# Maxima products ahead of the value product, later query copies, an earlier first modulation block

## The chip, the cores and the metric

The kernel runs on one core of a Trainium2 chip. Its time is the device time of one execution in microseconds (us); three executions of the kernel before gave 932.08, 932.74 and 933.2 us, median 932.74. Everything is computed in 32-bit floating point: where a matrix product runs on operands rounded for TensorE (type fp32r), the rounded-off rest is kept as a second operand and multiplied too.

Five engines run side by side, each through its own list of instructions in order: TensorE (PE) multiplies and transposes, VectorE (DVE) and ScalarE (ACT) work elementwise, GpSimd (POOL) too, and SyncE (SP) issues most transfers. They wait for one another by semaphores, which the kernel sets by hand.

## The reference

Two layers of a trunk over 512 latent tokens and 256 context tokens of width 1024. Per layer:

```
shift, scale, gate = split(silu(c) @ w_mod + b_mod)        # "modulation"; the same for the context with c_ctx
h = rms_norm(x, norm_w) * (1 + scale) + shift
u = h @ w_in                                               # 22 units of 128 columns
y_a = gated linear attention, 4 heads, chunks of 64, forwards and backwards
y_b = 6 heads of latent attention (MLA): 64 + 32 query and key columns, the 32 rotated
y_c = 6 query heads over 2 key heads (GQA, "grouped"), normed and rotated
x = x + gate * (concat(y_a, y_b, y_c) @ w_out)             # the context too, in layer 0
```

The latent queries of both softmax branches look at all 768 keys, the context's (layer 0 only) at 256. The softmax subtracts the largest score of each query. At the end the latent tokens are normed once more.

## The kernel before

**Tiles and stages.** The 768 tokens are six tiles of 128. At the start, each tile of x is loaded by SP, its sum of squares and the reciprocal root are made by ACT (`x_rstd`, L702 to L708), it is scaled by DVE (`xhat`, L1109), transposed by PE (L1652, eight transposes of 128x128), and copied out of the two banks by DVE and ACT (`turned_copy`, L1133 and L750). Between them stands the modulation: the small vectors are loaded into one tile and transposed by PE (L1657), ACT and DVE make silu of c (`condition`, L761 to L768 and L1069 to L1082), and PE multiplies it with blocks of 256 scale and 256 shift columns of w_mod (`mod`, L1616). The row that comes out is copied by ACT (`mod_rows`, L671), turned by PE (`mod_turn`, L1633), and made into coefficients by DVE (`mod_cols`, L1091 to L1102). Then ACT modulates the hidden columns (`modulate`, L727), DVE splits them into a rounded part and the rest (`split_hidden`, L1161, L1163), and PE multiplies with units of w_in (`unit_products`, L1671 to L1673). A unit is also split in two parts: ACT rounds it (`unit_high`, L721), DVE subtracts (`unit_low`, L1171).

Before the change the small vectors are transposed behind tile 0, the first modulation block stands behind tile 3, and all of `unit_low` is DVE's.

**Heads.** Behind the projections stand twelve heads per layer, 0 to 5 MLA, 6 to 11 GQA. PE goes through units of one key tile by 256 or 512 queries: eight in layer 0 (two for the context's queries, then six), six in layer 1. In each unit it makes the scores (MLA: L1941 to L1943; GQA: L1947 and L1949), and two units later the value product with the exponentials (`pv`, L1894, out of `flush`). ACT makes the exponentials (L1012). Between them PE makes scores of the next head for the maxima alone (`maxes`, L1859): from unit `MAX_FROM` on (3 in layer 0, 2 in layer 1), two per unit. DVE reduces each (L1462; L1454 for the context's), joins them into negated maxima (L1466), PE transposes these at the start of the next head (`max_rows`, L1865), and DVE writes them as extra rows of the queries (L1476), so that the score product subtracts them. A grouped head has no projection of its own, an MLA head has.

The gated linear attention goes along in the heads of each layer, one tile per head: its scores are made in unit `MAX_FROM` - 1 of the head before (`gla_a`) into two banks, and DVE copies them out under a mask (`a_mask`, L1333).

**Banks.** Products go into six banks of the accumulation memory, taken in turn by `open_`; each opening waits until the group that had the bank six openings earlier has been read. Value products have two banks of their own and open none of the six.

**ACT in a head.** It makes the exponentials in the order of the units. Behind the first it makes the reciprocal of the former head's denominators in two steps (`recip`, L968 and L970). For the grouped heads it copies the next head's queries and, at some heads, keys (`gqa_in`: part 0 the rounded queries, L944, and at every second head a copy for two heads, L948; part 1 the keys, L938, for the second grouped head; part 2 the queries for the other product, L952). Before the change part 0 stands before the first exponential of a head, parts 1 and 2 behind the first and the second. In heads 8 to 10 ACT also rounds pieces of w_out (L986).

The order of the work is written out by hand in the lists of the engines; there is no planner.

Of the kernel before, what the change touches and what calls it, by code (L numbers as in the profile page):

```python
# [26 lines left out]
ALU = mybir.AluOpType  # L27
# [198 lines left out]
def build(nc, tally, a, out):  # L226
    up, dma, at, let_go = tally.up, tally.dma, tally.at, tally.let_go
    with ExitStack() as ctx:
# [245 lines left out]
        def _(pool):  # L474
# [31 lines left out]
            for l in range(DEPTH):  # L506
                if l == 0:
                    swap_small(0)
                if l == 0:
                    pool.wait_ge(*at("filled", "mod", 0, 3))  # L510
                    layer_weights(0)
# [131 lines left out]
        def _(act):  # L643
# [68 lines left out]
            for l in range(DEPTH):  # L712
# [41 lines left out]
                if l == 0:  # L754
                    for t in range(TILES):
                        x_rstd(0, [t])
                        if t % 2 == 0 and t:
                            turned_copy(t - 1)
                        if t == 2:
                            act.wait_ge(*at("vec_turned"))  # L760
                            act.activation(ct[:, 0, :], vt[:, 0:16], ACT.Abs).then_inc(*up("cond_abs"))  # L761
                            act.wait_ge(*at("cond_abs"))
                            act.activation(ct[:, 0, :], ct[:, 0, :], ACT.Exp, scale=-1.0).then_inc(*up("cond_exp"))
                            act.wait_ge(*at("cond_exp"))
                            act.activation(ct[:, 0, :], ct[:, 0, :], ACT.Ln, bias=ones[:, 0:1]).then_inc(*up("cond_ln"))
                        if t == 3:
                            act.wait_ge(*at("cond_logsig"))
                            act.activation(ct[:, 1, :], ct[:, 1, :], ACT.Exp).then_inc(*up("cond_sig"))  # L768
# [231 lines left out]
                for h in heads:  # L1000
                    todo = [(q0, nq, kt) for q0, nq, nk in qbs(l) for kt in range(nk // P)]
                    more = h + 1 < len(heads)
                    if more:
                        if h + 1 < MLA_H:
                            head_in(h + 1)
                        elif h + 1 > MLA_H:
                            gqa_in(h + 1, 0)
                    for j, (q0, nq, kt) in enumerate(todo):
# [14 lines left out]
                        if h + 1 == MLA_H and j == 1:  # L1023
                            gqa_in(h + 1, 3)
                        if j < 2 and more and h + 1 > MLA_H:
                            gqa_in(h + 1, j + 1)
                        if j == 1 and h < len(out_tiles(l)):
# [36 lines left out]
        def _(dve):  # L1064
# [80 lines left out]
            for t in range(TILES):  # L1145
                if t == 3:
                    condition(1)
                xhat(0, t)
                if t:
                    turned_copy(t - 1)  # L1150
                if t == 2:
                    condition(0)
                if t == 3:
                    condition(2)
            turned_copy(TILES - 1)

            for l in range(DEPTH):
# [16 lines left out]
                if l == 0:  # L1174
                    mod_cols(0, 0)
                    unit_low(0)
                    split_hidden(0)
# [401 lines left out]
        def _(pe):  # L1579
# [64 lines left out]

            pe.wait_ge(*at("ident_in"))
            for t in range(TILES):
                pe.wait_ge(*at("xhat", 0, t))
                for half in range(2):
# [4 lines left out]
                    close(mm, "xr", t, half)  # L1653
                if t == 0:
                    pe.wait_ge(*at("vec_in"))
                    p = open_("vec")
                    close(pe.transpose(p[:, 0:V_ROWS], vec, ident[0:V_ROWS, 0:V_ROWS]), "vec")  # L1657
                if t == 3:
                    first_mod()

            def unit_products(p, l, item, c, ks):
                slot = UNITS[UNIT_OF[item]][1]
                pe.wait_ge(*at("w_split", l, UNIT_OF[item]))
                high, low = unit_parts(l, UNIT_OF[item])
# [30 lines left out]
            for l in range(DEPTH):  # L1695
# [216 lines left out]
                for h in heads:  # L1912
# [13 lines left out]
                    for j, (q0, nq, kt, nkt) in enumerate(units):  # L1926
# [31 lines left out]
                        if m and j == MAX_FROM[l] + (-1 if m[2] < 4 else 1):  # L1958
                            mod_turn(*m[1:])
                        flush(2)  # L1960
                        if j == 0 and h < len(tiles):
# [3 lines left out]
                        if j == MAX_FROM[l] - 1 and h + 1 < len(tiles):  # L1965
                            gla_a(tiles[h + 1])
                        if j >= MAX_FROM[l]:
                            maxes(groups[:2])
# [95 lines left out]
```

## Time and profile before

| | us |
|---|---|
| median of three runs | 932.74 |
| the profiled execution, its own time | 932.37 |
| its span, first to last instruction | 930.6 |
| PE busy | 889.3 |
| DVE busy | 532.6 |
| ACT busy | 414.7 |
| POOL busy | 170.0 |

The times of the rows are those of the profiled execution, counted from the start of its span. Busy time is time in which the engine works on an instruction; PEld is the loading of weights into TensorE, which goes beside its products. The granted clock is the share of TensorE's full clock of 2.4 GHz; 0.50 is 1.2 GHz. Its mean over the span is 0.99.

### The profile page before, as it was taken

How to read it: one execution, taken by the hardware profiler on the slowest of the kernel's cores; microseconds unless marked ns; L12 is line 12 of the kernel's file. 1: busy time of each engine (PE TensorE's matmuls, PEld its weight loads, DVE VectorE, ACT ScalarE, POOL GpSimd, SP SyncE). 2: the span in 40 equal slices, each digit the busy share in tenths (PEclk: the TensorE clock that was granted, in tenths of full speed). 3: DMA queues.
4: the chain of work that ended last, by engine and by line, in shares of the span. 5: the costliest groups of instructions: out<-in, count | busy, mean ns of one | idle time of the engine just before them, and what ended most of it. 6: DMA issues, size and time to landing. Idle time of an engine off the chain costs nothing.

```text
span 930.6 us, 12648 instructions
## 1 busy us (share of the span) xinstructions
PE 889.3 (96%) x4493; PEld 649.4 (70%) x4493; DVE 532.6 (57%) x941; ACT 414.7 (45%) x771; POOL 170.0 (18%) x200
## 2 busy tenths in 40 slices
PE   3799999999999999999999999999999999999995
PEld 2488889888766665655588888889775655545584
DVE  3545634534467677767624664743646877666624
ACT  5435534321344445667731744642314435546702
POOL 1031000001362223002162000000017211002240
PEclk8899999999999999999999999999999999999998
DMA  9842220320202222222027103411402000222032
GB/s 327 266 137 56 68 70 23 92 66 4 91 1 91 92 91 91 92 91 90 1 90 208 69 4 88 108 52 40 120 4 89 0 1 1 91 91 91 0 113 91
DMA packets 76252, 74.19 MB, mean 80 GB/s; under 512 B 6340, under 2 KB 64032, under 8 KB 76064
## 3 DMA queue, kind: packets, MB, share of 16 engines
q1 hardware_dynamic: 69776, 60.24, 21.1%
q0 software_dynamic: 4016, 12.77, 3.9%
q8 instruction: 39, 0.64, 0.3%
q10 hardware_dynamic: 2400, 0.38, 0.2%
q14 instruction: 21, 0.17, 0.1%
HBM read 69.18 MB, written 4.19 MB: 79 GB/s over the span
## 4 chain that ended last, share of the span: by engine, by line
PE 88%; DVE 5%; ACT 2%; issue 2%; POOL 1%; ACTq 1%; DVEq 0%; POOLq 0%
PE pv L1894 13%; PE bank L1671 10%; PE bank L1672 10%; PE bank L1673 10%; PE bank L1982 4%; PE bank L1980 4%; PE bank L1981 4%; PE bank L1859 4%; PE bank L1825 2%; PE bank L1941 2%; PE bank L1947 2%; PE bank L1943 2%; PE bank L1942 2%; PE bank L1719 2%; PE bank L1718 2%
## 5 line engine op out<-in xcount | busy, mean ns | idle before, releaser
L1671 PE MATMUL bank<-hA_parts,W_parts 128*128 128x512 f32 (+1 forms) x480 | 173.4, 361 | 4.9 <-DVE h_low_parts L1163 4.9
L1672 PE MATMUL bank<-hA_parts,W_parts 128*128 128x512 f32 (+1 forms) x496 | 173.6, 350 | 0.0
L1012 ACT ACTIVATE hA<-bank 128x512 f32<-128x512 f32 (+1 forms) x168 | 93.7, 563 | 128.5 <-PE bank L1943 76.2
L1462 DVE TENSOR_REDUCE mxp<-bank 128x1 f32<-128x384 f32 x192 | 95.7, 549 | 29.8 <-PE bank L1859 29.4
L1671 PEld LDWEIGHTS bank<-hA_parts,W_parts 128*128 128x128 f32 x480 | 91.1, 190 | 23.5 <-issue 11.4
L1673 PE MATMUL bank<-h_low_parts,W_parts 128*128 128x512 f32 (+1 forms) x300 | 105.2, 351 | 0.0
L1672 PEld LDWEIGHTS bank<-hA_parts,W_parts 128*128 128x128 f32 x496 | 94.1, 190 | 12.8 <-issue 1.7
L1894 PE MATMUL pv<-hA,vg 128*128 128x512 f32 (+1 forms) x168 | 81.6, 571 | 3.3 <-ACT hA L1012 3.3
L1171 DVE TENSOR_TENSOR W_parts<-W,W_parts 128x1024 fp32r<-128x1024 f32 x43 | 53.9, 1254 | 38.8 <-ACT W_parts L721 38.8
L1894 PE MATMUL pv<-hA,h_low 128*128 128x512 f32 (+1 forms) x144 | 68.5, 556 | 0.0
L721 ACT ACTIVATE W_parts<-W 128x1024 fp32r<-128x1024 f32 x43 | 45.4, 1056 | 38.8 <-DMA W<-in_w_in 38.3
L1673 PEld LDWEIGHTS bank<-h_low_parts,W_parts 128*128 128x128 f32 x300 | 57.0, 190 | 7.7
L1981 PE MATMUL bank<-W_parts,hA_parts 128*128 128x512 f32 x160 | 62.3, 389 | 0.0
L813 ACT ACTIVATE tz<-bank 128x512 f32<-128x512 f32 (+1 forms) x24 | 12.6, 526 | 83.9 <-PE bank L1673 83.9
L702 ACT ACTIVATE tz<-XA 128x1024 f32<-128x1024 f32 x16 | 16.9, 1055 | 72.8 <-DVE XA L1559 72.8
L1218 DVE SCALAR_TENSOR_TENSOR YA<-tz,bank 128x512 f32<-128x512 f32 (+1 forms) x24 | 14.3, 597 | 57.3 <-ACT tz L813 57.3
L1859 PE MATMUL bank<-W_parts 96*128 96x384 f32 (+1 forms) x108 | 44.9, 493 | 1.2 <-DVE glaqk L1333 0.5
L1433 DVE SCALAR_TENSOR_TENSOR hA<-pv,hA 64x512 f32<-64x512 f32 (+1 forms) x36 | 21.5, 598 | 41.7 <-ACT hA L970 41.4
L1554 DVE TENSOR_TENSOR rt<-bank,cqkv 128x512 f32<-128x512 f32 x20 | 13.7, 687 | 54.5 <-DMA XA<-in_x 19.0
L1673 PE MATMUL bank<-rounded,W_parts 128*128 128x512 f32 (+1 forms) x120 | 41.8, 348 | 0.0
L1894 PEld LDWEIGHTS pv<-hA,vg 128*128 128x128 f32 x168 | 29.5, 190 | 16.3 <-ACT hA L1012 6.8
L533 POOL TENSOR_TENSOR XA<-XA,con 128x512 f32<-128x512 f32 x10 | 12.2, 1221 | 148.8 <-DVE XA L1315 78.3
(288 smaller groups left out, 1897.3 us busy)
## 6 DMA issues: line engine op xcount, KB each, us to landing
W<-in_w_in SPq DMA_DIRECT2D x39, 512.0 KB, 4.0
W<-in_w_mod SPq DMA_DIRECT2D x8, 1024.0 KB, 6.5
W<-in_w_mod SPq DMA_DIRECT2D x4, 2048.0 KB, 7.9
W<-in_w_out SPq DMA_DIRECT2D x4, 2048.0 KB, 7.9
gqk<-in_w_mod SPq DMA_DIRECT2D x4, 768.0 KB, 9.2
cqkv<-in_w_mod SPq DMA_DIRECT2D x4, 768.0 KB, 9.2
XA<-in_x SPq DMA_DIRECT2D x4, 512.0 KB, 7.2
XA<-in_x POOLq DMA_DIRECT2D x4, 512.0 KB, 6.5
```

Of the source, the lines that this page charges most:

```text
L721: act.activation(unit_parts(l, u)[0], w_units[:, 0, slot], ACT.Copy).then_inc(*up("w_high", l, u))
L1012: act.activation(prob[slot % 4][:, 0:nq], ps("sc", l, h, q0, kt)[:, 0:nq], ACT.Exp, scale=MLA_SCALE if h < MLA_H else GQA_SCALE)\
L1171: dve.tensor_tensor(rest, w_units[:, 0, slot], high.bitcast(F32), ALU.subtract)\
L1462: dve.tensor_reduce(mxp[:, t, half:half + 1], ps("mx", l, h, q0, t, half)[:, 0:384], AX, ALU.max).then_inc(*up("part_max", l, h, q0, t, half))
L1671: pe.matmul(p[:, 0:c[1]], high[:, k, :], h_hi[:, k, toks], start=(k == 0), stop=False)
L1672: pe.matmul(p[:, 0:c[1]], low[:, k, :], h_hi[:, k, toks], start=False, stop=False)
L1673: mm = pe.matmul(p[:, 0:c[1]], high[:, k, :], h_lo[k][:, toks], start=False, stop=(k == KD - 1))
L1859: close(pe.matmul(p[:, 0:n], q[:, t * P:t * P + P], k[:, n * half:n * half + n], start=True, stop=True), "mx", l, h, q0, t, half)
L1894: mm = pe.matmul(pv_banks[i % 2][:, 0:nq], v, prob[sl % 4][:, 0:nq], start=(kt == 0), stop=(kt == nkt - 1))
L1980: pe.matmul(p[:], hi, w_hi[n][k], start=(k == 0), stop=False)
L1981: pe.matmul(p[:], hi, w_lo[:, i % 2, k, :], start=False, stop=False)
L1982: mm = pe.matmul(p[:], lo, w_hi[n][k], start=False, stop=(k == KD - 1))
```

## The change

1. In every unit from `MAX_FROM` on, the two maxima products stand ahead of the unit's value product, in all heads.
2. ACT's `gqa_in` for the next grouped head moves back by one exponential: part 0 behind the first, part 1 behind the second, part 2 behind the third.
3. The small vectors are transposed ahead of tile 0; the steps of `condition` move one or two tiles forwards on ACT and DVE; the first modulation block stands behind tile 2. The split of the first unit of layer 0 moves from DVE to POOL.

```diff
@@ POOL @@
                     swap_small(0)
+                    high, rest = unit_parts(0, 0)
+                    pool.wait_ge(*at("w_high", 0, 0))
+                    pool.tensor_tensor(rest, w_units[:, 0, 0], high.bitcast(F32), ALU.subtract)\
+                        .then_inc(*up("first_split"))
@@ ACT, first tiles @@
-                        if t == 2:
+                        if t == 1:
                             act.wait_ge(*at("vec_turned"))
...
-                        if t == 3:
+                        if t == 2:
                             act.wait_ge(*at("cond_logsig"))
@@ ACT, heads @@
                         if h + 1 < MLA_H:
                             head_in(h + 1)
-                        elif h + 1 > MLA_H:
-                            gqa_in(h + 1, 0)
...
-                        if j < 2 and more and h + 1 > MLA_H:
-                            gqa_in(h + 1, j + 1)
+                        if j < 3 and more and h + 1 > MLA_H:
+                            gqa_in(h + 1, j)
@@ DVE, first tiles @@
-                if t == 3:
+                if t == 2:
                     condition(1)
                 xhat(0, t)
+                if t == 0:
+                    condition(0)
+                if t == 2:
+                    condition(2)
                 if t:
                     turned_copy(t - 1)
-                if t == 2:
-                    condition(0)
-                if t == 3:
-                    condition(2)
@@ DVE @@
                     mod_cols(0, 0)
-                    unit_low(0)
                     split_hidden(0)
@@ PE, first tiles @@
+            pe.wait_ge(*at("vec_in"))
+            p = open_("vec")
+            close(pe.transpose(p[:, 0:V_ROWS], vec, ident[0:V_ROWS, 0:V_ROWS]), "vec")
             for t in range(TILES):
...
-                if t == 0:
-                    pe.wait_ge(*at("vec_in"))
-                    p = open_("vec")
-                    close(pe.transpose(p[:, 0:V_ROWS], vec, ident[0:V_ROWS, 0:V_ROWS]), "vec")
-                if t == 3:
+                if t == 2:
                     first_mod()
...
-                pe.wait_ge(*at("w_split", l, UNIT_OF[item]))
+                pe.wait_ge(*(at("first_split") if (l, item) == (0, "small") else at("w_split", l, UNIT_OF[item])))
@@ PE, heads @@
+                        first = j >= MAX_FROM[l]
+                        if first:
+                            maxes(groups[:2])
+                            groups = groups[2:]
                         flush(2)
...
-                        if j >= MAX_FROM[l]:
+                        if j >= MAX_FROM[l] and not first:
                             maxes(groups[:2])
                             groups = groups[2:]
```

## Rows read from the trace of the kernel before

**Rows 1.** The page's busy times: us, share of the span, instructions.
```profile
PE 889.3 (96%) x4493; PEld 649.4 (70%) x4493; DVE 532.6 (57%) x941; ACT 414.7 (45%) x771; POOL 170.0 (18%) x200
```

**Rows 2.** Who PE waited for: us in total, times, longest.
```profile
PE bank L1865 <- DVE nmx L1466: 3.9, 14, 0.3
```

**Rows 3.** Order of time, first stage: start, us, engine, line, operation [idle before].
```profile
16.28 0.22 ACT L761 ACTIVATE ct<-vt 128x16 f32<-128x16 f32 x1 [0.96 <-DVE vt L1069]
...
16.99 1.04 ACT L702 ACTIVATE tz<-XA 128x1024 f32<-128x1024 f32 x1
...
28.26 0.16 DVE L1102 SCALAR_TENSOR_TENSOR mA<-mA,vt 128x4 f32<-128x4 f32 x1
```

**Rows 4.** The first block's last transfer: issue in ns and at, then its landing.
```profile
L442 SPq DMA_DIRECT2D glaqk<-in_w_mod x1: 3745/3745/3745, 7.0 to 7.0; - x1
...
DMA to landing us min/median/max: 11.8/11.8/11.8
```

**Rows 5.** Stretches: us, PE busy (matmuls), granted clock, DMA share, GB/s.
```profile
18.50:19.50 1.00, 0.00 (x0) 0.50 1.05 370
...
21.53:25.20 3.67, 3.67 (x18) 0.50 1.09 352
```

**Rows 6.** POOL's line L616: ns shortest/median/longest, first and last start, forms.
```profile
L616 POOL TENSOR_TENSOR W_parts<-W,glav_parts x6: 1267/1277/1657, 428.2 to 853.2; 128x512 fp32r<-128x512 f32 x6
```

**Rows 7.** Order of time, DVE's L1438 beside POOL and alone.
```profile
332.39 1.04 POOL L533 TENSOR_TENSOR XA<-XA,con 128x512 f32<-128x512 f32 x1 [14.33 <-PE bank L1805]
...
332.76 1.21 DVE L1438 TENSOR_TENSOR YA<-hA,YA 64x512 f32<-64x512 f32 x1
...
433.20 0.68 DVE L1438 TENSOR_TENSOR YA<-hA,YA 64x512 f32<-64x512 f32 x1
```

**Rows 8.** The chain of waits, layer 0, heads 3 and 9: start, us, what.
```profile
326.29 0.11 PE bank L1865
...
435.21 0.35 PE bank L1859 x2
...
439.41 0.86 PE pv L1894 x2
...
441.77 0.27 PE bank L1865
```

**Rows 9.** Order of time, mask copies (DVE L1333) and loads for maxima (PEld L1859).
```profile
269.58 1.73 DVE L1333 COPY_PREDICATED glaqk<-con,bank 128x256 f32<-128x256 int32 x4
...
721.43 1.73 DVE L1333 COPY_PREDICATED glaqk<-con,bank 128x256 f32<-128x256 int32 x4
...
723.58 0.19 PEld L1859 LDWEIGHTS bank<-W_parts 96*128 96x128 f32 x1 [0.24 <-issue]
...
741.07 1.72 DVE L1333 COPY_PREDICATED glaqk<-con,bank 128x256 f32<-128x256 int32 x4
...
742.90 0.19 PEld L1859 LDWEIGHTS bank<-W_parts 96*128 96x128 f32 x1 [0.62 <-issue]
...
758.04 1.72 DVE L1333 COPY_PREDICATED glaqk<-con,bank 128x256 f32<-128x256 int32 x4
```

**Rows 10.** Order of time, layer 1, head 6: a maxima product.
```profile
816.43 0.88 PE L1859 MATMUL bank<-wuq_parts,hA_parts 96*128 96x384 f32 x2 [0.25 <-DVE mxp L1462]
```

**Rows 11.** Order of time, layer 0, start of head 9: ACT, and PE's value product.
```profile
427.98 0.83 ACT L944 ACTIVATE hA_parts<-gqk 64x768 fp32r<-64x768 f32 x1
...
430.69 0.38 ACT L1012 ACTIVATE hA<-bank 128x256 f32<-128x256 f32 x1 [1.14 <-PE bank L1949]
...
431.72 0.63 ACT L970 ACTIVATE hA<-hA 64x512 f32<-64x512 f32 x1
...
432.81 0.70 PE L1894 MATMUL pv<-hA,vg 128*128 128x256 f32 x2 [0.47 <-ACT hA L1012]
```

**Rows 12.** Order of time, layer 1, start of head 9.
```profile
848.75 1.10 PE L1894 MATMUL pv<-hA,vg 128*128 128x512 f32 x2
...
849.25 0.63 ACT L970 ACTIVATE hA<-hA 64x512 f32<-64x512 f32 x1
```

## The prediction

> **What bounds the kernel now.** I read the busy shares first: TensorE (PE) is busy 96% of the span, ScalarE (ACT) 45%, VectorE (DVE) 57% [rows 1]. So a step on DVE, ACT or GpSimd (POOL) counts only where PE waits for it. The second view is who waited for whom: of PE's few waits in the heads the largest is for the negated maxima, 3.9 us in 14 places [rows 2]. The third is the order in time at such a place, the fourth the first 30 us, where PE stands still most. The reader should look for one thing: after each matmul that opens a bank, what has to release it, and how long before that had been done.
>
> **First stage.** The work until the coefficients of the first two column blocks are ready ends at 28.26 + 0.16 = 28.42 us [rows 3]. The change puts the first modulation block behind the third token tile. I follow the queues. ACT's three conditioning steps (0.71 us from the start of the first to what follows, 16.28 to 16.99 [rows 3]) now stand before tile 2's statistics, which end at 14.75; tile 2 is scaled by 15.55 and turned by 17.1. The conditioning is then ready at about 15.9, but the block's weights are not: their last transfer is issued at 7.00 us and takes 11.8 us to land, 18.8 us [rows 4]. The block so starts at 18.85, not 21.53. Behind it in PE's queue stand the transposes of tile 3, behind those ACT's copy of tile 3, behind that the statistics of tile 5 (1.7 us), its scaling on DVE (0.75), its transposes (1.4) and the turn of the row of coefficients. How long the block takes hangs on the clock. Before, PE was idle from 16.25 to 19.6; the granted clock was 0.50 (1.2 GHz) from 18.5 on, and the block took 3.67 us at it [rows 5]; at the full 2.4 GHz it would take half, 1.85. The new order has a gap too, 17.1 to 18.85, and I can't exclude either level. At full clock: block to 20.7, tile 3's first half turned at 21.4, ACT's copy to 22.1, statistics of tile 5 to 23.75, scaling 24.5, transposes 26.0, coefficients at 27.45: a gain of 1.0 us. At half clock until about 21.9: block to 22.15, tile 5's statistics to 25.2, scaling 25.95, transposes 27.4, coefficients 28.75: a loss of 0.3 us.
>
> The split of the first weight unit goes from DVE to POOL. On DVE it stood beside ACT's first modulation (1.3 us), so its 1.22 us were off the path and their removal gives nothing. On POOL 128x512 of the same operation takes 1.3 us [rows 6], so 128x1024 about 2.6 us: from the end of ACT's copy of the unit (25.3 or 26.8) to 27.9 or 29.4, ahead of the first product, which came 3.2 us behind the coefficients. But DVE's coefficient steps fall into it, and two of them read two operands from the on-chip memory. The nearest rows are of the heads: DVE's gating product took 1.21 us beside a POOL product of 1.04 us, against 0.68 elsewhere [rows 7]: 0.5 us more. Bounds: nothing, and the rest of POOL's 2.6 us. I take 0.5 to 0.8 us, which makes the stage +0.5 us, the mean of about -0.3 and +1.1. POOL's next step in the queue waits for a later block anyway, so nothing else stands behind. Transposing the small vectors first costs nothing: before, they followed tile 0 at once without a wait, at 13.25 us, and if they land by 11.7 they fit into PE's idle time; at worst tile 0 waits 1.5 us, most of it covered by the statistics of tile 2.
>
> By the Trainium skill (SBUF — State Buffer, SBUF: two separate sides) the pair of ports that DVE and POOL share is locked for a whole instruction, and a DVE operation with two inputs in SBUF waits for it. The trace's 1.21 us against 0.68 agrees. By that rule the coefficient steps could wait for the full rest of POOL's product, and the stage would come out 1.5 to 2.5 us later; the sum above doesn't use it.
>
> **Maxima ahead of the value product: what it gains.** At the end of a grouped head PE does the last value product (0.86 us for both passes), then the last two maxima products (0.35), one more value product, and then waits for DVE's two reductions and the joining one before it can transpose the maxima: that transpose ends at 441.77 + 0.27 = 442.04 us. Without a wait it would end at 439.41 + 0.86 + 0.35 + 0.86 + 0.11 = 441.59, the 0.11 from a head in which nothing is late [rows 8]. So 0.44 us in each of the 14 places. The change puts the maxima 0.86 us earlier, more than enough. In seven of them (next head 5, 6, 8 and 9 of layer 0; 6, 8 and 9 of layer 1) nothing speaks against it: 7 x -0.44, less about 0.1 in a head with little slack: -3.0 us.
>
> **What it costs.** A maxima product needs a bank, and the banks go round in six. The bank of the second pair after the local attention's scores (tile A, mask copies at L1333) is freed by those copies. In layer 1, head 1 they run from 741.07 to 742.79, and PE loads the second product of the pair at 742.90, 0.11 us later [rows 9]: PE already waits. Today the 0.86 us of the value product stand in front of this wait and cover it. Now they stand behind it, so that PE reaches the pair 0.86 us earlier, waits until the same moment, and has the 0.86 us still to do. DVE's mask copies don't come earlier: the chain before them starts at the transposed maxima of the head's start, and DVE has hardly a gap in it. The same holds in layer 0, heads 0 and 4, and layer 1, heads 1 and 2 (of the five mask copies concerned the first starts at 269.58 and the last at 758.04) [rows 9]. In layer 1, head 0 the banks are free at 721.43 + 1.73 = 723.16 and the load was at 723.58 [rows 9]; wanted 0.86 earlier, and with 0.12 for the signal, that is 0.56 us. In the other heads with masks the slack is more than 0.98 us. Nothing later in these heads waits, so nothing gives it back: 4 x 0.86 + 0.56 = +4.0 us. The bounds are 0 (if DVE's chain shortened by as much) and 5.2.
>
> Where DVE is behind with the reductions themselves, the same happens: in layer 1, head 6 PE's product at 816.43 waits 0.25 us for a reduction already [rows 10]. For the three heads of this kind (next head 7 of layer 0, 5 and 7 of layer 1) I get 0, +0.24 and +0.38 us with the 0.44 counted: +0.6 us.
>
> **The grouped heads' copies.** Today ACT copies the next head's queries before the first exponential, at 427.98, while it waits 1.14 us for the scores [rows 11]: they are free. Moved behind it, they stand behind the two steps of the reciprocal and before the second exponential, where ACT has no gap: the reciprocal ends at 431.72 + 0.63 = 432.35, and the value product of the second unit waits for that exponential already (432.81, 0.47 us idle) [rows 11]. Each copy adds 0.74 us from start to start in layer 0, about 0.53 in layer 1. In heads 7 and 8 a modulation block of 1.85 us on PE covers it, in head 6 another copy moves out of the way. In heads 9 and 10 nothing does. Layer 0, head 9 (two copies, 1.48 us): second exponential done at 434.25 instead of 432.8; then ACT, with four weight copies of 0.6 us and a second reciprocal in the same units, is late for the exponentials 4 and 5 as well; following both queues the transpose of the maxima comes 1.15 us late, the 0.44 counted. Head 10 (one copy): +0.55. In layer 1 the maxima start a unit earlier, right behind the third scores, and now need a copy that is not there yet: in head 9 PE would want them at 848.75, when the value product starts, but the reciprocal ends at 849.25 + 0.63 and the copy takes 0.61 more, 850.5 [rows 12]. Of these 1.75 us about half is given back, as ACT and DVE were late there before: +0.85, and +0.7 in head 10. Together +3.2 us; bounds -0.7 (the copies hidden, a part of the 0.44 kept) and +5.
>
> **Sum.** +0.5 - 3.0 + 0.6 + 4.0 + 3.2 = +5.3 us, on the profiled execution's 932.37 us 937.7, and 0.37 us more on the median of the three runs (932.74): 938.0 us.
>
> **Rivals.**
> - Faster: the mask copies free their banks earlier. Place: the five heads with masks [rows 9]. If the DVE chain that ends in the masks gets 0.86 us shorter in the new order, the waits cost nothing and all 14 places give 0.44: -6.2 + 3.2 (copies) - 0.3 (first stage at full clock) = -3.3, 929.4 us. It decides from masks that end 1 us before the load. For it: the maxima of the former head end earlier. Against it: the chain starts at PE's own transpose. 0.15.
> - Hardly anything: ACT hides the copies and the first stage gains its 1.0 us: -3.0 + 0.6 + 4.0 - 1.0 = +0.6, 933.3 us. For it: ACT is busy less than half the time over the span; against: the waits at 432.81. 0.17.
> - More: the port lock of the first stage costs 2 us more than I take, and the second head with two copies (layer 1, head 9) gives nothing back and costs as much as the first, another 1 to 2 us: 942 us. 0.10.
> - My forecast, 935 to 941 us: 0.58.
>
> **Numbers.** The range 931.5 to 941.5 leaves out most of the first rival and half of the third. About 0.2% (1.9 us) is what can be told from no change: faster 0.15, same 0.17, slower 0.68.
>
> **What would show it.** First modulation block near 18.85 us, coefficients between 27.4 and 30; PE waiting for L1333's copies some 0.9 us longer in five heads; the waits for the negated maxima gone in at least seven of 14 places; ACT's second exponential 0.7 to 1.5 us later after the first in heads 9 and 10. It is wrong if PE's waits for the mask copies stay at 0.2 to 0.4 us, or if the value product in heads 9 and 10 waits no longer than before.

## The result and the profile of the changed kernel

The changed kernel takes 941.11 us (median of four runs, 939.05 to 942.70) against 932.64 us (932.08 to 933.20) for the one before: ratio 1.0095, 95% interval 1.0082 to 1.0108. It is slower by 8.5 us, by the ratio by 8.9; the ratios are taken over all runs and aren't the quotients of the medians, so the two ways of counting differ by up to 0.8 us. The forecast was slower by 5.3 (938.0 us, range to 941.5). The sign holds, and the size is 3.1 us short. The range holds only by the median: the ratio times the forecast's own base is 932.74 x 1.0095 = 941.6, and the profiled execution took 941.61, both just past its end.

The page of the changed kernel, its span, busy times (us, share, instructions) and the granted clock in tenths, slice by slice of 23.5 us:

```profile
span 939.7 us, 12648 instructions
...
PE 890.8 (95%) x4493; PEld 652.4 (69%) x4493; DVE 531.9 (57%) x940; ACT 413.8 (44%) x771; POOL 172.3 (18%) x201
...
PEclk8899999999999999999999999999999999999998
```

Against [rows 1] PE's busy time grew by only 1.5 us, though the span grew by 9.1: the rest went into waits. Who PE waited for (us, times, longest):

```profile
PE bank L1859 <- ACT hA_parts L948: 7.4, 6, 1.7
...
PE bank L1859 <- DVE glaqk L1334: 3.4, 9, 0.6
...
PE pv L1617 <- DMA glaqk<-in_w_mod: 2.8, 1, 2.8
...
PE pv L1894 <- ACT hA L1014: 1.3, 3, 0.6
```

The wait of [rows 2], 3.9 us in 14 places, is gone from this list. In its place stand waits of maxima products (L1859): for a grouped head's query copy on ACT (L948, L944 before) and for the mask copies (L1334, L1333 before).

Every head has one transpose of its maxima on PE (L1865). Its start in the two profiled executions, subtracted, gives the shift at that point, and the difference of two shifts is what the head in between gained or lost. "At" is the head whose transpose it is (layer.head), so the row 0.10 is what head 9 of layer 0 lost; "forecast" is the term of the sum. The first row holds all that comes ahead of the heads. For it one execution says little: the five kernels below whose first stage is as before, with the same instructions in it, have -0.92, -0.90, -0.21, +0.04 and +0.59 in this row. All other rows repeat from trace to trace within some hundredths where nothing was changed, but for 1.0 and 1.1, which shift by up to 0.4 against each other.

```
at                shift gained over the head before      forecast
0.0               +2.43 (the first stage)                +0.5
0.1, 0.5          +0.84, +0.38 (= 0.84 mask - 0.46)      +0.86, +0.42
0.6, 0.8, 0.9     -0.46, -0.46, -0.45                    -0.44 each
1.6, 1.8, 1.9     -0.24, -0.46, -0.49                    about -0.44 each
1.0, 1.1          -0.36, +0.92: together +0.56           +0.56
1.2, 1.3          +0.86, +0.87                           +0.86 each
0.7, 1.5, 1.7     +0.42, +0.44, +0.42                    0, +0.24, +0.38
0.10, 0.11        +2.24, +0.66 (copies)                  +1.15, +0.55
1.10, 1.11        +0.82, +0.82 (copies)                  +0.85, +0.70
others            -0.03 to +0.01                         0
sum               +9.15                                  +5.3
```

The masks (3.97 us together) and the gains (-3.02) came as forecast. Three terms are too small: the first stage by 1.9, the end of head 9 of layer 0 by 1.1, the three heads in which VectorE is behind by 0.7. These 3.7 us make up the miss between the two profiled executions but for 0.2 (941.61 - 932.37 = 9.24 against 5.3, so 3.9).

### The profile page after: what moved, and what is told of

The parts are those of the page before. It is cut to its first block, busy times and chain, and to the rows that moved or that the text cites. A ratio compares the mean times of both kernels' runs of the same rounds, so it can differ in the third digit from the quotient of the medians.

```text
span 939.7 us, 12648 instructions
## 1 busy us (share of the span) xinstructions
PE 890.8 (95%) x4493; PEld 652.4 (69%) x4493; DVE 531.9 (57%) x940; ACT 413.8 (44%) x771; POOL 172.3 (18%) x201
## 4 chain that ended last, share of the span: by engine, by line
PE 89%; DVE 4%; ACT 3%; issue 2%; DMA 1%; SPq 1%; POOL 0%; ACTq 0%; DVEq 0%
PE pv L1894 14%; PE bank L1671 10%; PE bank L1672 10%; PE bank L1673 10%; PE bank L1859 4%; PE bank L1986 4%; PE bank L1984 4%; PE bank L1985 4%; PE bank L1825 3%; PE bank L1941 2%; PE bank L1718 2%; PE bank L1719 2%; PE bank L1717 2%; PE bank L1947 2%; PE bank L1871 2%
## 5 line engine op out<-in xcount | busy, mean ns | idle before, releaser
L1014 ACT ACTIVATE hA<-bank 128x512 f32<-128x512 f32 (+1 forms) x168 | 93.4, 563 | 136.4 <-PE bank L1943 80.5
L1894 PE MATMUL pv<-hA,vg 128*128 128x512 f32 (+1 forms) x168 | 79.4, 570 | 1.3 <-ACT hA L1014 1.3
L1894 PE MATMUL pv<-hA,h_low 128*128 128x512 f32 (+1 forms) x144 | 67.8, 556 | 0.0
L1894 PEld LDWEIGHTS pv<-hA,vg 128*128 128x128 f32 x168 | 29.7, 191 | 14.2 <-issue 10.8
L1717 PE MATMUL bank<-W_parts,hA_parts 128*128 128x384 f32 x96 | 35.9, 374 | 0.0
```

Of the source, the lines that this page charges most:

```text
L1014: act.activation(prob[slot % 4][:, 0:nq], ps("sc", l, h, q0, kt)[:, 0:nq], ACT.Exp, scale=MLA_SCALE if h < MLA_H else GQA_SCALE)\
L1717: pe.matmul(o, h_hi[:, k, tok], high[:, :, k, :], start=(k == 0), stop=False)
L1894: mm = pe.matmul(pv_banks[i % 2][:, 0:nq], v, prob[sl % 4][:, 0:nq], start=(kt == 0), stop=(kt == nkt - 1))
```

## Experiments: the three parts alone

Four kernels, each the kernel before with one edit. They ran on one chip, beside 16 runs of the kernel before (931.69 us).

**The first stage alone.** Nothing is changed in the heads; in the first stage all that the change has, the core of it:

```
+ pool.wait_ge(*at("w_high", 0, 0)); pool.tensor_tensor(rest, w_units[:, 0, 0], high, ALU.subtract)
- unit_low(0)                                            # DVE
+ close(pe.transpose(... vec ...), "vec")                # PE, now ahead of the token tiles
- if t == 3: first_mod()                                 # PE
+ if t == 2: first_mod()
...                                                      # ACT, DVE: conditioning one tile earlier
```

> The kernel before with the first stage's edits alone (block 0 between tiles 2 and 3, small vectors turned first, split of the first unit on POOL). Theory (the parts add, as the head starts of the two traces lay them out): the first head's maxima rows go from 351 us of the span to some 2.4 later and nothing later changes, so 932.6 + 2.4 = 935.0. Rival (the stage's loss in the changed kernel came from the clock, and the clock's stretches fall differently here): 931.7 to 933.2.

Measured: 933.22 us, 11 runs from 931.59 to 934.54, ratio 1.0010 (1.0001 to 1.0019). That is +0.9 us by the ratio, +1.5 by the medians. It is less than the theory's 2.4 and inside the rival's range but for 0.02: the loss is not a fixed one of 2.4. The runs scatter more than the effect is large, and the profiled one, 931.59, is the fastest of the 11; the last section has the scatter.

**The maxima alone.**

```
  if m and j == MAX_FROM[l] + (-1 if m[2] < 4 else 1): mod_turn(*m[1:])
+ first = j >= MAX_FROM[l]
+ if first:
+     maxes(groups[:2]); groups = groups[2:]
  flush(2)
  ...
- if j >= MAX_FROM[l]:
+ if j >= MAX_FROM[l] and not first:
```

> The kernel before with the maxima ahead of the value product in all units of all heads, nothing else. Theory: the waits for the masks' banks and their order cost 0.86 in five heads (+4.3), seven heads give back 0.44 each (-3.1), three heads in which VectorE is behind lose 0.4 each (+1.2), four two-copy heads give 0.44 each (-1.7), so +0.7 us: 933.3. Rival 1 (the copies' heads gain nothing because ScalarE is what they wait for): +2.5, 935.1. Rival 2 (the mask waits exist only beside the later first stage): -4, 928.6.

Measured: 934.77 us, ratio 1.0027 (1.0015 to 1.0038), +2.5 us. Outside the four grouped places the head steps are those of the changed kernel to within 0.03 us: +0.86 at 0.1, +0.40 at 0.5, -0.46, +0.41, -0.46 at 0.6 to 0.8, +0.87 and +0.86 at 1.2 and 1.3; only 1.0 and 1.1 together are +0.41 instead of +0.56. Rival 2 is out. At the four places of the grouped heads the steps are -0.10, -0.07, +0.15 and -0.08: the four gains of 0.44 that my sum had counted there don't come. That is rival 1's number, but not its reason. ScalarE isn't what these heads wait for, as the kernel with the last unit alone (below) gains 0.44 in each of them with the same ScalarE. What eats the gain in head 9 of layer 0 stands in the last unit but one, where VectorE's reductions (L1462) run without a gap and the pair needs a bank that they still read (kernel with the maxima alone, PE):

```profile
438.37 0.88 PE L1859 MATMUL bank<-wukv_parts,hA_parts 96*128 96x384 f32 x2
439.08 1.02 PE L1894 MATMUL pv<-hA,vg 128*128 128x512 f32 x2
```

The pair holds PE for 0.71 us until the value product; where no bank is missing it does so for 0.35.

**The copies alone.** Three copies of the next grouped head, each one exponential later.

```
-     elif h + 1 > MLA_H:
-         gqa_in(h + 1, 0)          # ahead of the first exponential
...
- if j < 2 and more and h + 1 > MLA_H: gqa_in(h + 1, j + 1)
+ if j < 3 and more and h + 1 > MLA_H: gqa_in(h + 1, j)
```

> The kernel before with the grouped heads' three copies behind the first three exponentials instead of ahead of the first and behind two. Theory: it costs in L0 heads 9 and 10 and L1 heads 9 and 10 alone, together 4.5 us less what the order of the maxima gave there, so +4 us: 936.6, with the waits of the maxima on the query copy of up to 1.7 us in the trace. Rival 1 (the maxima were not ahead here, so VectorE's reduces and the copies overlap and the late copy is hidden): +1 at most, 933.6. Rival 2: the same +6.3 without the 0.44 counted, 939.

Measured: 936.79 us, ratio 1.0046 (1.0033 to 1.0059), +4.3 us. It falls on the four places foreseen, +2.94, +0.60, +0.75 and +0.43, and on one that wasn't, +0.25 at 0.8. Both rivals fail. PE, start of head 9 of layer 0 (start, us, engine, line, operation, idle before): where the value product waited 0.47 us [rows 11] it waits

```profile
434.24 0.70 PE L1892 MATMUL pv<-hA,vg 128*128 128x256 f32 x2 [1.93 <-ACT hA L1010]
```

1.46 us more, the two copies' price (1.48 in the forecast). The other half of the 2.94 is the clock, below.

The three parts measured alone add up to 0.9 + 2.5 + 4.3 = 7.7 us of the 8.9, all by ratios. In the traces the parts' head rows add up to 6.6 us of the changed kernel's 6.7; what doesn't add is the first row (-0.4 against +2.43).

**The maxima ahead in the last unit only.** `first = j + 1 == len(units)` instead of `j >= MAX_FROM[l]`.

> The kernel before with the maxima ahead of the value product in the last unit of each head alone; in the other units they stay behind it. Theory: the last pair of maxima is what ends the head's wait, so each of the heads whose rows of maxima wait for VectorE gains 0.44 (up to 14 heads with the two-copy ones), and no maxima reach a bank that the masks hold, because the bank ring moves by one group only at the last unit: -4 to -6 us, 927 to 929. Rival (the gain comes from all pairs being earlier, since VectorE works them off back to back): -1 to 0, 931.6 to 932.6.

Measured: 926.55 us (925.38 to 927.69), ratio 0.9942 (0.9929 to 0.9954): 5.4 us faster than before by the ratio. Twelve of the 14 places gain 0.41 to 0.46 us, two 0.33, and the mask heads 0.03 at most. The timeline of PE in head 9 of layer 0 shows the new end:

```profile
437.20 0.52 PE L1859 MATMUL bank<-wukv_parts,hA_parts 96*128 96x384 f32 x2
437.56 1.88 PE L1894 MATMUL pv<-hA,vg 128*128 128x512 f32 x4
439.28 0.27 PE L1865 MATMUL bank<-con,nmx 128*6 128x128 f32 x1
```

Two value products (four matmuls, 1.88 us) now cover VectorE's last two reductions and the joining one; the transpose follows without a wait, where before one covered and 0.44 us was left open [rows 8].

## Experiments: which unit pays, which part of the first stage pays

These four ran on a second chip beside 33 runs of the kernel before (932.25 us).

**Maxima ahead except where the masks hold the banks.** `first = j >= MAX_FROM[l] and not (h + 1 < len(tiles) and j == MAX_FROM[l] + 1)`.

> The kernel before with the maxima ahead of the value product, except in the one unit (fifth of L0, fourth of L1) of the heads with a next tile, in which they take the banks that the masks hold. Theory: the four or five mask steps of 0.86 go (the step of head 1, L0, and of heads 1, 2, 3, L1, is 0.0 to 0.1 in the traces), the rest stays as in the kernel with all of them ahead: 934.8 - 4.3 = 930.5. Rival (the banks only move the wait to the next unit, since VectorE is behind for several units there): 933 or more.

Measured: 930.68 us, ratio 0.9987 (0.9978 to 0.9996). The five mask steps are -0.02, 0.00 (-0.46 with its gain), -0.01 (1.0 and 1.1 together), 0.01 and 0.00: one unit of each mask head carries the whole cost. The two products that wait in head 1 of layer 1, with all maxima ahead (changed kernel), PE:

```profile
748.22 0.41 PE L1859 MATMUL bank<-W_parts 96*128 96x384 f32 x1 [0.42 <-DVE glaqk L1334]
...
749.02 0.41 PE L1859 MATMUL bank<-W_parts 96*128 96x384 f32 x1 [0.39 <-DVE glaqk L1334]
```

0.42 + 0.39 = 0.81 us of waiting, just about the value product that used to stand in front.

**Ahead in the last two units.** `first = j + 2 >= len(units)`.

> The kernel before with the maxima ahead of the value product in the last two units of each head. Theory (what counts is when the last pair is filled; the earlier pairs are read by VectorE in time either way): the same as with the last unit alone, 926.5 within 0.5. Rival 1 (VectorE is what is behind, so earlier pairs earlier gain more): 925. Rival 2 (bank order and ScalarE's exponentials: each unit in which the maxima go ahead makes the value product one pair later, and three heads lose 0.4 each as with all of them ahead): 927.5 to 928.

Measured: 930.78 us, ratio 0.9984 (0.9975 to 0.9993): 4.2 us slower by the medians than with the last unit alone, 3.9 by the ratios, more than any of the three expectations had. It loses +0.41 each at 0.7, 1.5 and 1.7, and has no gain at 0.10, 0.11, 1.10 and 1.11. PE's timeline, head 6 of layer 1, first this kernel, then the one with the last unit alone:

```profile
814.13 0.88 PE L1859 MATMUL bank<-wuq_parts,hA_parts 96*128 96x384 f32 x2 [1.10 <-DVE mxp L1462]
```

```profile
812.67 0.88 PE L1859 MATMUL bank<-wuq_parts,hA_parts 96*128 96x384 f32 x2 [0.27 <-DVE mxp L1462]
```

It is [rows 10] again (0.25 us): the last pair but one needs a bank that a reduction still reads. Put ahead, it meets that wait without its cover of 0.86 us. In the grouped heads the same wait is shorter: in head 9 of layer 0 the pair holds PE from 435.26 to 435.98, 0.72 us instead of 0.35, which eats most of the 0.44. In the last unit the pair's early start is worth more than the cover, because the joined maximum is what the transpose waits for next; in the unit before, nothing waits for the pair, and the wait is laid bare. So in this kernel the pair goes ahead in one unit, the last.

**The first stage with the split left on VectorE**, the other edits of the stage kept:

```
- pool.tensor_tensor(rest, w_units[:, 0, 0], high, ALU.subtract).then_inc(*up("first_split"))
+ unit_low(0)                                            # DVE, as before
```

> The first stage's edits alone, but with the split of the first unit left on VectorE. Theory (of the stage's cost, the split on POOL holds the shift's add up, 1.09 us instead of 0.16 in two traces): the add takes 0.16 us here, but VectorE has the 1.22 us of the split back before the first hidden part; so the stage moves by -0.9 + (0 to 1.2): 932.3 to 933.2 against 933.2 with the split on POOL, and the time still scatters by 1.5 to 3 us with the granted clock of the first 40 us. Rival (the split on POOL is a gain, because VectorE's 1.22 us goes from the chain to the first products): 934 or more.

Measured: 931.06 us, ratio 0.9994 (0.9985 to 1.0002), below both, and not to be told from the kernel before.

**The first stage with block 0 behind tile 3**, the other edits of the stage kept:

```
- if t == 2: first_mod()
+ if t == 3: first_mod()
```

> The first stage's edits alone, but block 0 of the modulation behind tile 3 as before; the small vectors first, the condition's steps earlier and the split on POOL stay. Theory (the block moved up waits for its weights, which land no earlier, and holds tile 3's transposes up behind itself, so the move gains nothing but shifts where the clock is low): 931.5 to 932.7, below the 933.2 of the same with the move. Rival (the move gains and the split costs): 933.5 to 934.5.

Measured: 929.81 us, ratio 0.9974 (0.9965 to 0.9983). Against 933.22 that is 3.4 us: the costliest edit of the first stage. The theory had allowed down to 931.5 only; the other edits of the stage together are a gain. The two traces, this one and the one of the stage alone, both have the block at full clock and one later stretch of 3.4 us at half. In them the coefficients are ready at 25.78 and 27.80 us, so about 2.0 us is what the order in the queues costs. That the other 1.4 us of the timed runs is the clock is argued, not shown.

## Experiments: the causes put together

Four kernels beside 15 runs of the kernel before (932.12 us).

**The changed kernel with block 0 back behind tile 3** (one line).

> The changed kernel with block 0 of the modulation back behind tile 3, all else as changed. Theory (what the forecast missed in the first stage is the move of the block: ScalarE's copy of tile 3, and behind it its sums for tile 5, wait for transposes that are queued behind the block): the 3.4 us between the two kernels with the first stage's edits alone (933.2 and 929.8) go here too, 941.1 - 3.4 = 937.7. Rival (the stage and the heads' changes meet in the clock, not in the queues): 939.5 to 941.

Measured: 937.35 us, ratio 1.0054 (1.0041 to 1.0067), 0.35 us from the theory. That is closer than the trace deserves: the start of the first transpose goes from +2.43 to -3.07 against before, 5.5 us, and 1.65 us of it is lost again near the end of layer 1 (+2.47 at 1.11 instead of +0.82), in a second stretch at half clock.

**Vectors and conditioning early, block and split as before.**

> The first stage's edits with block 0 behind tile 3 and the split of the first unit left on VectorE, so what remains is the small vectors' turn ahead of the tiles and the condition's steps one tile earlier. Theory (the split on POOL holds the shift's add up, 1.28 us in the trace instead of 0.16): 929.8 - 1.0 = 928.8. Rival (VectorE's 1.22 us of the split comes back ahead of the first hidden part's cast): 929.6 to 930.5.

Measured: 928.72 us (927.97 to 928.77), ratio 0.9965 (0.9953 to 0.9978). The theory's value to 0.1 us.

**The changed kernel with the maxima ahead in the last unit only.**

> The changed kernel with the maxima ahead of the value product in the last unit of each head only. Theory (the parts add): 941.1 - (934.8 - 926.6) = 932.9. Rival (with the copies late the maxima of the first units wait less for the query copy when they stand behind the value product, so more comes back): 931.0 to 932.0.

Measured: 930.86 us, ratio 0.9984 (0.9975 to 0.9993): 2 us below the theory, 0.14 below the rival's lower end. The rival has the number, but its reason isn't borne out. The maxima products' wait for the query copies does fall, from 7.4 us in six places to

```profile
PE bank L1859 <- ACT hA_parts L948: 2.1, 3, 0.7
```

but the value products' wait for the exponentials (L1894 for L1014) grows from 1.3 us to 4.9. In the traces the distance from the changed kernel to this one is 10.9 us, and from the kernel with all maxima alone to the one with the last unit alone 8.3. Of the 2.5 us between the two, 1.06 stands in the first row, 1.00 at 0.10, where the changed kernel has a stretch at half clock and this one none, and 0.46 at 1.11. So only at 1.11 do the two edits in the grouped heads plainly make each other worse (+0.82, where the parts alone add up to +0.35); most of the rest is the clock.

**The best version**: early vectors and conditioning, nothing else of the first stage; copies as before; maxima ahead in the last unit.

> Vectors and condition early, block 0 behind tile 3, split on VectorE, copies as before, maxima ahead in the last unit of each head only. Theory: 931.9 - 3.2 (first stage) - 5.3 (maxima) = 923.4. Rival (a faster first stage shifts the clock's low stretch into the products behind it and gives a part back): 924.5 to 925.5.

Measured: 923.18 us (922.47 to 923.29), ratio 0.9908 (0.9894 to 0.9921). It beats both kernels: 9 us below the one before, 18 below the changed one. Of the rival (a part given back to the clock) nothing shows.

## Where the forecast was right, and where it failed

The sign was forecast for the right reason; the size was not. The step that failed is the price of PE's half clock. In the first stage the sum took the mean of two levels, +0.5 us, where the trace has +2.43; in head 9 of layer 0 it counted waits alone, +1.15, where the trace has +2.24, 1.64 of them from a stretch at half clock that the forecast didn't have. A smaller third term, the three heads with VectorE behind, was +0.6 and measured 1.28.

**The sign** hangs on masks and copies, and both were read from waits that [rows 9, 11, 12] already showed: a wait is covered by the work queued in front of it, and moving the work behind it lays it bare. The mask term was 4.0 and is 3.97. The maxima's gain was 0.44 a place and is 0.45 to 0.49 in six of seven places, 0.24 at 1.6. The first rival (mask copies free their banks earlier) is out: the mask heads lose 3.97 us here and 3.86 with the maxima alone, as they should if the banks come free no earlier. Its 929.4 us was also added up wrongly: the 0.44 of the four grouped places stands both in its -6.2 and in the 3.2 of the copies.

**First stage, +0.5 forecast, +2.43 in the profiled execution, +0.9 in the timed runs of it alone.** What failed is "At half clock until about 21.9", and the mean. I had the block start cold and warm up under way, and took this case and the one at full clock for equally likely (their mean is +0.4, not +0.5). The changed kernel, all engines:

```profile
19.25 2.78 PE L1617 MATMUL pv<-gqk,sc 128*32 128x512 f32 x10 [2.80 <-DMA glaqk<-in_w_mod]
...
22.82 2.88 PE L1656 MATMUL bank<-con,YA 128*128 128x128 f32 x16
23.98 0.60 ACT L754 ACTIVATE hA<-bank 128x512 f32<-128x512 f32 x1 [5.68 <-PE bank L1656]
24.47 1.05 ACT L706 ACTIVATE tz<-XA 128x1024 f32<-128x1024 f32 x1
...
27.69 2.34 POOL L511 TENSOR_TENSOR W_parts<-W,W_parts 128x1024 fp32r<-128x1024 f32 x1 [7.62 <-ACT W_parts L725]
...
28.97 1.09 DVE L1100 TENSOR_TENSOR mB<-modc,vt 128x4 f32<-128x4 f32 x1
...
30.16 0.16 DVE L1104 SCALAR_TENSOR_TENSOR mA<-mA,vt 128x4 f32<-128x4 f32 x1
```

The block starts 0.4 us later than forecast, after 2.80 us of idle PE, and runs at the half clock to its end (3.6 us); the clock rose at 24.7, not at 21.9. ACT stands idle for 5.68 us, because tile 3's transposes are behind the block. The coefficients are ready at 30.3 us, 28.42 before: 1.9 us later, where the forecast's two cases with the split on POOL were -0.3 and +1.1. The other 0.5 of the 2.43 arises behind them, with the clock again at half from 31.6 to 38.4 us, 6.8 us, against 3.4 in the kernel before. The queue was read rightly, including who waits for whom; the clock's share was guessed at the near end. How large that share is, three traces with this same first stage show (columns as in [rows 5]: stretch, us, busy PE, PEld, DVE, ACT, POOL, then the granted clock; the kernel with the first stage alone, then the changed one):

```profile
0.00:28.43 28.43, 10.98 (x69) 8.26 (x69) 11.93 (x23) 14.96 (x36) 6.08 (x15) 1.00 1.01 331
28.43:60.00 31.57, 28.16 (x170) 20.15 (x171) 17.00 (x31) 13.91 (x22) 4.79 (x6) 0.95 0.60 194
```

```profile
0.00:28.43 28.43, 12.79 (x69) 8.82 (x69) 10.12 (x19) 14.45 (x34) 4.43 (x15) 0.88 1.01 330
28.43:60.00 31.57, 25.77 (x154) 18.17 (x152) 15.68 (x33) 13.33 (x21) 4.74 (x5) 0.89 0.56 187
```

The third is the changed kernel with the last unit alone:

```profile
0.00:28.43 28.43, 11.94 (x69) 8.25 (x69) 11.17 (x21) 14.56 (x34) 5.39 (x15) 0.94 1.00 332
28.43:60.00 31.57, 26.60 (x161) 18.73 (x162) 16.34 (x33) 14.43 (x22) 5.45 (x7) 0.95 0.56 186
```

Their shifts at the first transpose are -0.74, +2.43 and, for the third, +0.83 us: the same instructions up to there, 3.2 us apart, in the order of their clocks. In the first of them the block runs at full clock and the coefficients are ready at 27.8 us, 0.3 before what the forecast's case at full clock gives with the split on POOL (27.45 + 0.65).

And the whole question was put too narrowly. I weighed the move of the block against the kernel before, and it looked like nothing; I did not weigh it against the same edits without the move. There the time in which PE waits for the block's weights goes to tile 3's transposes. The first stage with block 0 behind tile 3, PE:

```profile
17.70 1.09 PE L1658 MATMUL bank<-con,YA 128*128 128x128 f32 x8 [1.09 <-DVE YA L1113]
19.54 1.48 PE L1619 MATMUL pv<-gqk,sc 128*32 128x512 f32 x10 [0.75 <-DMA glaqk<-in_w_mod]
```

Block 0 starts 0.3 us later than in the changed kernel. Over all traces with the early conditioning it starts at 18.8 to 19.5 us behind tile 3 and at 18.8 to 19.3 behind tile 2: it waits for its weights either way, and moving it up gains nothing. But tile 3's chain isn't behind it, and in all four traces with it behind tile 3 it runs at the full clock, in those with it behind tile 2 in one of four. The timed runs make a square (differences against before, worked out from the ratios, each to about 1 us, so that the move of the block, 2.7 and 3.3, is clear of it):

```
                     split on VectorE    split on POOL
block behind tile 3       -3.3 us           -2.4 us
block behind tile 2       -0.6 us           +0.9 us
```

**The split on POOL.** I took 0.5 to 0.8 us; the square gives 0.9 and 1.5, with uncertainties of 1.4 and 1.2, so the price rests on the traces. In five traces with the split on POOL the shift's add on DVE takes 1.08 to 1.29 us, against 0.16 in all without it, and in the changed kernel it ends with POOL's product: 27.69 + 2.34 = 30.03 against 28.97 + 1.09 = 30.06 above. By the Trainium skill (SBUF — State Buffer, SBUF: two separate sides) the one who comes second to the ports that the two engines share waits for the other's whole instruction; the trace agrees to 0.03 us. The lock cost 1.09 - 0.16 = 0.93 us here and not 2 more than I took, as the rival "More" had it, because POOL had begun 1.28 us before the add did.

**Copies, +3.2 forecast, +4.54.** Three of four places are within 0.12, and that is luck. The forecast had +0.55, +0.85 and +0.70 with a gain of 0.44 in each, so copies of 0.99, 1.29 and 1.14; the copies alone cost 0.60, 0.75 and 0.43, and the gains of the maxima alone are -0.07, +0.15 and -0.08. Two errors cancel, and at 1.11 another 0.47 comes only with both edits together. Head 9 of layer 0 was to cost 1.15 and cost 2.24, and its waits are smaller than derived: from the transpose to the third unit's first score product (L1947) it is 431.91 to 437.26 in the changed kernel and 429.28 to 433.59 before, 1.04 us more. With the 0.44 that comes back at its end that is +0.6. The other 1.64 is the clock. Stretches around the stall in the changed kernel, then in the changed kernel with the last unit alone (us, busy PE, ..., granted clock):

```profile
437.75:441.16 3.41, 3.41 (x8) 2.19 (x7) 1.58 (x5) 3.30 (x7) 1.27 (x1) 0.50 0.00 0
```

```profile
433.75:437.16 3.41, 3.41 (x14) 2.24 (x14) 1.59 (x5) 3.31 (x7) 1.28 (x1) 1.00 0.00 0
```

In the same time PE gets through 8 products instead of 14. The second kernel has a stall of 1.94 us at this place, no shorter than the others' (0.80 + 0.58 in the changed kernel, 1.93 with the copies alone), and its clock stayed at 1.00; its step is +0.89, not +2.24. So the stall does not bring the fall with certainty. Of four traces with the copies late, three have such a stretch of 3.4 us in the middle of the heads (one has a second, near the end of layer 1, where its step is 2.47 instead of 0.82); of ten traces with the copies early none has. An estimate for a stretch at half clock with PE busy throughout is half of its 3.41 us, 1.7 us; the two places give 1.64 and 1.65. The timed runs of the copies alone fit: two at 934.7 us with a mean clock of 0.994, three at 936.8 to 937.7 with 0.990 and 0.991. What decides whether a given stall is followed by such a stretch was not settled.

**The three heads with VectorE behind, +0.6, and 1.28.** I let the waits there grow by 0.44, 0.68 and 0.82 us. They are laid bare in full in each of the three: 0.86, less the 0.44 that comes back, is 0.42, and +0.42, +0.44 and +0.42 were measured; the wait of [rows 10] itself goes from 0.27 to 1.10 us with the last two units ahead. The same wait, shorter, takes the four gains of the grouped heads, which I had counted and which the kernel with the maxima alone does not show (-0.10 to +0.15).

**The sum.** 1.9 + 1.1 + 0.7 = 3.7 of 3.9 us missed in the profiled executions. The 1.9 is time at the half clock and the waits behind it, of which the forecast's sum took half of the milder case, and about 0.3 us more of the port lock. Part of it belongs to this one execution, as the timed runs of the stage alone lose only 0.9 to 1.5. The 1.1 is a fall of the clock in the midst of the heads, of which the forecast has no word.

## What to carry to other kernels

When work is moved ahead of other work, look for the wait behind it that it used to cover; move only the piece whose end somebody waits for next, here the last pair of 5 (or 4). Weigh each edit of a change against the same change without it, not only against the kernel before: the early vectors and conditioning (tried only together) and the last pair were good here, and were hidden by the moved block, the split on POOL, the late copies and the maxima ahead in the other units. Where PE is idle for a microsecond or two before a busy stretch, let the sum's range take in both clock levels for all of what follows, and judge such a stage by many timed runs, not by one trace.

## What the hardware showed that I had not expected

- A stall of PE of 0.8 and 0.6 us (changed kernel) or 1.93 us (copies alone), in the midst of work that had run at 1.00 for 400 us, was followed by 3.4 us at the granted clock 0.50, and one of 1.94 us in a fourth kernel by none. The start shows the same without any difference in the instructions: in the six kernels whose first stage is as before, the clock came back to 1.00 at 22.7 to 25.9 us (22.66, 23.82, 23.99, 25.28, 25.32, 25.94), and the coefficients were ready at 27.2 to 28.9. The Trainium skill (TensorE: Matmul & The Clock Gate, Part 1: The HAM clock gate) says that the point at which the clock rises varies by half a microsecond either way from one run to the next. These traces agree that it varies, and here it does by 3.3 us.
- The timed runs cluster. The kernel with the first stage alone ran at 931.6 to 931.8 us five times, at 933.2 to 933.4 five times and once at 934.5, with mean granted clocks of 0.995 to 0.996, 0.994 and 0.992. The steps of about 1.5 us are close to the 1.7 of one stretch at half clock more or less; that these lie in the first 40 us, as in the traces, is argued, since timed runs have no trace. The five runs of the best version lay within 0.8 us.
- VectorE's add of 128x4 elements took 1.09 us beside a POOL product of 2.34 us, seven times its 0.16. What such a small instruction pays is the rest of POOL's.
